# Two layers of a hybrid diffusion step, written out without a barrier, with the second layer's first modulation units moved into the first layer

## The chip, the cores and the metric

The kernel runs on one core of a Trainium2 chip. The metric is the device time of one execution in microseconds, the median of the runs. One launch computes everything.

## The reference, cut to what matters

Two token streams, a prompt of 128 tokens and a sample of 512, go through DEPTH = 2 layers with model width 1024. They share all weights, and each stream has its own condition vector, from which every layer derives 9 modulation vectors. The kernel keeps the 640 tokens of both side by side.

```python
def modulation(cvec, l):
    m = jax.nn.silu(cvec) @ w_mod[l] + b_mod[l]          # 9 vectors of 1024
    return m.reshape(cvec.shape[0], N_MOD, D_MODEL)

def layer(x, p, l, mod, ctx):
    g = p['norm_w'][l]
    def half_ffn(x, j, s):
        h = modulate(rmsnorm(x, g[2 * s]), mod[:, 3 * s], mod[:, 3 * s + 1])
        y = swiglu(h, p['ffn_w1'][l, j], p['ffn_w3'][l, j], p['ffn_w2'][l, j])
        return x + 0.5 * mod[:, 3 * s + 2][:, None] * rmsnorm(y, g[2 * s + 1])
    x = half_ffn(x, 0, 0)
    h = modulate(rmsnorm(x, g[2]), mod[:, 3], mod[:, 4])
    y, new = token_mixing(h, p, l, ctx)                  # four mixers, then w_out
    x = x + mod[:, 5][:, None] * rmsnorm(y, g[3])
    return half_ffn(x, 1, 2), new
```

The modulation depends on the condition and on w_mod[l] alone, not on x. The first feed-forward half needs its first three vectors (shift, scale, gate).

## The kernel before, in words

Everything is held feature-major: `xT` is 8 tiles of 128 features by 640 tokens. A norm of x goes like this. ScalarE (ACT) squares the eight tiles, PE sums them over the partitions with a matrix of ones (`sums`, L533 or L538), ACT takes the reciprocal root (Ln, then Exp, both at L932, the line of its helper `fn`), and `norm_in` on VectorE (DVE) scales each tile (L1310) and splits it into an upper and a lower part (ACT, then L1317). `norm_out` (L1334, L1337) scales the result of a block and adds it to x, tile by tile.

The weights come in units, one transfer each, numbered in the order in which PE uses them. There are three kinds:

- A modulation unit is 1024 KB of w_mod, 256 of its columns. PE uses it as it is (`mod`, L512, 16 matmuls with 2 output rows); the DVE copies the rows to `mrow` (L1270), PE turns them (`mod_turn`, L522, 4 matmuls), and the DVE adds the bias and stores two columns (`mod_cols`, L1276). 36 units make the nine vectors of a layer, 12 make the first three.
- An up unit (w13, 1024 KB) holds the gate and value weights of 128 hidden features. GpSimd (POOL) first splits each weight into an upper and a lower part (`split`, L454 and L459); PE makes three products of every pair (L501 to L503), 96 matmuls in all; ACT takes the Silu of the gate (L932), the DVE multiplies by the value (L1346) and splits (L1349).
- A down unit (w2, 704 KB) is treated alike and gives one output tile, copied (L1356) in group 0 and added (L1358) in group 1.

SyncE (SP) issues all weight transfers in the order of the units (`load`, L392). They go to a ring of two slots, and slot n % 2 is free once the unit two before has been split by POOL, or, for a modulation unit, used by PE. Each layer's first 12 modulation units have a ring of their own, `first_raw`, which lies in the memory of the second buffer of split weights. The split weights have two buffers as well.

Each half of the feed-forward (`ffn(s, j)`, s = 0 for the first, s = 2 for the last) runs in two groups of 11 up units and 8 down units. In the first half (s = 0) a modulation unit stands before, between and behind the up units, 12 in a group, for the last 24 of the layer. In the last half (s = 2) there are none.

The order of work at the start of a layer: the parameters `par` are loaded, then the 12 first modulation units run alone, with the squares of x beside them; after eight of them the scales are there, and `norm_step` runs between the last four. Then the products of the first up unit begin, one k tile at a time as `h_ready` rises (`first_products`).

Both layers are one piece of code in `nc.Fori(0, DEPTH)` (L376). Each engine's part of a layer is in one `nc.Block`; at the end of an iteration all semaphores are cleared and all engines meet in a barrier:

```python
        with nc.Fori(0, DEPTH) as l:
            with nc.Block() as block:
                ...
            nc.sync.sem_clear(range(nums[0], nums[-1] + 1))
            nc.all_engine_barrier()
```

Of the kernel before, what the change touches and what calls it, by code (L numbers as in the profile page):

```python
# [28 lines left out]
P = 128  # L29
# [6 lines left out]
DEPTH = 2  # L36
# [30 lines left out]
U_ALL = U_FFN[2] + 2 * GRP_U[2]  # L67
assert U_ALL == 133
# [3 lines left out]
MODS = set(range(MOD_U))  # L72
for _g in range(2):
    _n = U_FFN[0] + _g * GRP_U[0]
    MODS |= {_n + 2 * _m for _m in range(MOD_U)}
SPLIT = [n for n in range(U_ALL) if n not in MODS]
# [38 lines left out]

def build(nc, I, O):
    ctx = ExitStack()
    with ctx:
        def sb(name, words):
            return ctx.enter_context(nc.sbuf_tensor(name, [P, words], FP))  # L120

        sems = []

        def sem(name):
            s = ctx.enter_context(nc.semaphore(name))
            sems.append(s)
            return s
# [104 lines left out]
        rpb_loaded = sem("rpb_loaded")  # L232
        wa2_loaded = sem("wa2_loaded")


        first_loaded = [sem(f"first{i}_loaded") for i in range(SLOTS)]
        loaded = [sem(f"slot{i}_loaded") for i in range(SLOTS)]
        pool_hi = sem("pool_hi")
        split_done = sem("split_done")
        mrow_ready = sem("mrow_ready")  # L240
        mtr_done = sem("mtr_done")
        turn_begun = sem("turn_begun")
        split_begun = sem("split_begun")
        a_hi = sem("a_hi")
        a_lo = sem("a_lo")
        acc_add = sem("acc_add")
        y_scaled = sem("y_scaled")
        y_norm = sem("y_norm")
        dense_done = sem("dense_done")
        dense_act = sem("dense_act")  # L250
        dense_dve = sem("dense_dve")
        dense_hi = sem("dense_hi")
        spilled = sem("spilled")
        reloaded = sem("reloaded")
        y_sum = sem("y_sum")
        cat_read = sem("cat_read")
        h_hi = sem("h_hi")
        cat_hi = sem("cat_hi")
        cat_split = sem("cat_split")
        init_loaded = sem("init_loaded")  # L260
        st_out = sem("st_out")
        na_out = sem("na_out")
        m_out = sem("m_out")
        unit_done = sem("unit_done")
        unit_evac = sem("unit_evac")
        par_loaded = sem("par_loaded")
        mod_ready = sem("mod_ready")
        gate_ready = sem("gate_ready")
        sq_ready = sem("sq_ready")
        ss_done = sem("ss_done")  # L270
        rstd_ready = sem("rstd_ready")
        hmul_ready = sem("hmul_ready")
        h_ready = sem("h_ready")
        silu_done = sem("silu_done")
        x_ready = sem("x_ready")
        gate_pre = sem("gate_pre")
        gate_sp = sem("gate_sp")
        gate_log = sem("gate_log")
        gate_exp = sem("gate_exp")
        gate_t = sem("gate_t")  # L280
        gate_cols = sem("gate_cols")
        apre_done = sem("apre_done")
        asp_done = sem("asp_done")
        ad_ready = sem("ad_ready")
        ae_ready = sem("ae_ready")
        aqk_ready = sem("aqk_ready")
        akt_done = sem("akt_done")
        akt_ready = sem("akt_ready")
        lg_ready = sem("lg_ready")
        lg_sp = sem("lg_sp")  # L290
        dec_ready = sem("dec_ready")
        rot_ready = sem("rot_ready")
        rt_done = sem("rt_done")
        rt_evac = sem("rt_evac")
        qd_ready = sem("qd_ready")
        kt_ready = sem("kt_ready")
        u_done = sem("u_done")
        t_done = sem("t_done")
        s_ready = sem("s_ready")
        p_done = sem("p_done")  # L300
        wl_done = sem("wl_done")
        w_ready = sem("w_ready")
        a_done = sem("a_done")
        o_done = sem("o_done")
        ot_done = sem("ot_done")
        act_gate = sem("act_gate")
        nrm_in = sem("nrm_in")
        nrm_out = sem("nrm_out")
        fin_ready = sem("fin_ready")
        cat_t = sem("cat_t")  # L310
        cat_done = sem("cat_done")
        na_s = sem("na_s")
        na_read = sem("na_read")
        na_max = sem("na_max")
        na_e = sem("na_e")
        na_n = sem("na_n")
        na_pt = sem("na_pt")
        na_ptc = sem("na_ptc")
        na_o = sem("na_o")
        na_oc = sem("na_oc")  # L320
        cond_ready = sem("cond_ready")
        y_out = sem("y_out")
# [7 lines left out]
        slot = lambda n: n % SLOTS  # L330
        use = lambda n: 16 * ((n if n < MOD_U else n - MOD_U) // SLOTS + 1)
        SD = lambda n: PARTS * (SPLIT.index(n) + 1)
# [3 lines left out]
        R = lambda g, z, t: (g * 2 + z) * NT + t + 1  # L336
# [11 lines left out]
        def slot_ap(n, words):  # L348
            ring = first_raw if n < MOD_U else raw
            return ring[:, slot(n) * SLOT_W:slot(n) * SLOT_W + words]  # L350

        def arrival(n):
            return (first_loaded if n < MOD_U else loaded)[slot(n)]

        def split_ap(n, words):
            return w_split[SPLIT.index(n) % SLOTS][:, :, 0:words]


# [17 lines left out]
        with nc.Fori(0, DEPTH) as l:  # L376
            with nc.Block() as block:

                @block.sync
                def _(sp):  # L380
                    sp.dma_start(par[:, :], I["par"][l]).then_inc(par_loaded, 16)

                    def load(n, words, src, i=0, du=2, ds=2):


                        if MOD_U <= n < MOD_U + SLOTS:
                            pass
                        elif n - SLOTS in SPLIT:
                            sp.wait_ge(split_done, i * (ds * PARTS) + SD(n - SLOTS))
                        else:  # L390
                            sp.wait_ge(unit_done, i * du + UD(n - SLOTS))
                        sp.dma_start(slot_ap(n, words), src).then_inc(arrival(n), 16)  # L392

                    for u in range(2):
                        load(u, SLOT_W, I["w_mod"][l, u])
                    load(MOD_U + 1, SLOT_W, I["w13"][l, 0])
                    with sp.Fori(0, MOD_U // 2 - 1) as i:
                        for u in range(2):
                            load(2 + u, SLOT_W, I["w_mod"][l, i * 2 + (2 + u)], i)
                    load(MOD_U, SLOT_W, I["w_mod"][l, MOD_U])  # L400
                    for s, j in ((0, 0), (2, 1)):
                        for grp in range(2):
                            n = U_FFN[s] + grp * GRP_U[s]
                            f0 = j * FT + grp * GF_T
                            if s == 0:
                                m0 = MOD_U * (1 + grp)
                                if grp:
                                    load(n, SLOT_W, I["w_mod"][l, m0])
                                    load(n + 1, SLOT_W, I["w13"][l, f0])
                                load(n + 2, SLOT_W, I["w_mod"][l, m0 + 1])  # L410
                                with sp.Fori(0, GF_T - 1) as i:
                                    load(n + 3, SLOT_W, I["w13"][l, i + (f0 + 1)], i, ds=1)
                                    load(n + 4, SLOT_W, I["w_mod"][l, i + (m0 + 2)], i)
# [22 lines left out]
                @block.gpsimd  # L436
                def _(pool):
                    def split(n, words, i=0, du=2):


                        pool.wait_ge(arrival(n), i * (8 * du) + use(n))
                        k = SPLIT.index(n)
                        if k == 1:
                            pool.wait_ge(unit_done, UD(MOD_U - 1))
                        if k >= SLOTS and SPLIT[k - SLOTS] in AFTER:
                            pool.wait_ge(dense_done, AFTER[SPLIT[k - SLOTS]])
                        elif k >= SLOTS:
                            pool.wait_ge(unit_done, i * du + UD(SPLIT[k - SLOTS]))
                        pool.sem_inc(split_begun, 1)
                        w, src = split_ap(n, words), slot_ap(n, words)  # L450
                        step = words // PARTS
                        for q in range(PARTS):
                            at = slice(q * step, (q + 1) * step)
                            nc.gpsimd.tensor_scalar(w[:, 0, at], src[:, at], 1.0, 1.0, ALU.mult, ALU.mult)\  # L454
                                .then_inc(pool_hi, 1)
                        for q in range(PARTS):
                            at = slice(q * step, (q + 1) * step)
                            pool.wait_ge(pool_hi, i * (2 * PARTS) + (k * PARTS + q + 1))
                            nc.gpsimd.tensor_tensor(w[:, 1, at], src[:, at], w[:, 0, at].bitcast(FP), ALU.subtract)\  # L459
                                .then_inc(split_done, 1)  # L460

                    for s in (0, 2):
                        step = 2 if s == 0 else 1
                        for grp in range(2):
                            n = U_FFN[s] + grp * GRP_U[s] + step - 1
# [6 lines left out]
                            n = U_FFN[s] + (grp + 1) * GRP_U[s] - KT  # L472
# [14 lines left out]
                @block.tensor  # L487
                def _(pe):
# [1482 lines left out]
```

## Time and profile before

| | us |
|---|---|
| median of 3 runs (3286.01 to 3288.61) | 3286.97 |
| profiled execution | 3288.13 |
| its span, first to last instruction | 3286.3 |
| PE matmuls busy | 2971.4 (90%) |
| POOL busy | 1365.5 (42%) |
| DVE busy | 985.0 (30%) |
| ACT busy | 582.0 (18%) |
| mean granted TensorE clock, of full speed | 0.941 |

The profiled execution lasted 1.83 us longer than its span. Times below are in us from the start of the span. The start of layer 1 lies about in its middle: the engines leave the loop's barrier at about 1647. The granted clock is TensorE's; 1.00 is 2.4 GHz, 0.50 is 1.2 GHz.

### The profile page before, as it was taken

The page shows a single profiled execution, that of the slowest core. Times are in us where ns is not written, and L with a number is a line of the kernel's source. Part 1 is how long each engine was busy: PE and PEld are TensorE (multiplying, and loading weights), DVE is VectorE, ACT ScalarE, POOL GpSimd, SP SyncE. Part 2 cuts the span into 40 slices and gives each one's busy share as a digit, 9 for nine tenths or more (in the row PEclk, how much of TensorE's full clock was granted, in tenths as well). Part 3 has the DMA queues.
Part 4 walks back from the last instruction along what each step waited for, and adds up shares of the span by engine and source line. Part 5 has one row for each costly group of instructions (what it writes and reads, how often), then busy time and mean ns, then how long its engine had stood idle before and what let it go on. Part 6 is the DMA issues. An engine that isn't in the chain of part 4 may idle for free. (4 is left out here: it accounts for less than half of the span.)

```text
span 3286.3 us, 51128 instructions
## 1 busy us (share of the span) xinstructions
PE 2971.4 (90%) x20984; PEld 2807.7 (85%) x20984; DVE 985.0 (30%) x1589; ACT 582.0 (18%) x976; POOL 1365.5 (42%) x1556
## 2 busy tenths in 40 slices
PE   6999999798878899999779999997988787999996
PEld 3999999698877799999749999997988776999996
DVE  3110111624646531111231101116245465310112
ACT  2000001312213420011120000013121135110111
POOL 1445445333322345655314454463332223455553
PEclk7999999899888899999969999998998888999998
DMA  6332332211102111221163323322111021112111
GB/s 260 128 124 87 128 128 88 93 59 44 44 26 90 52 52 65 83 77 61 35 219 132 123 100 128 125 80 86 55 46 41 27 90 52 56 63 93 68 66 59
DMA packets 46378, 281.98 MB, mean 86 GB/s; under 512 B 5088, under 2 KB 10720, under 8 KB 20512
## 3 DMA queue, kind: packets, MB, share of 16 engines
q1 hardware_dynamic: 39024, 259.46, 22.2%
q10 hardware_dynamic: 7216, 20.60, 1.7%
q8 instruction: 96, 1.57, 0.2%
q14 instruction: 42, 0.34, 0.0%
HBM read 270.07 MB, written 9.97 MB: 85 GB/s over the span
## 5 line engine op out<-in xcount | busy, mean ns | idle before, releaser
L454 POOL TENSOR_SCALAR wsplit<-raw 128x512 fp32r<-128x512 f32 (+2 forms) x776 | 441.0, 595 | 1880.2 <-issue 856.3
L501 PE MATMUL ps<-h,wsplit 128*128 128x320 f32 (+1 forms) x3488 | 1103.4, 316 | 63.5 <-DVE rstd L1346 25.6
L502 PE MATMUL ps<-h,wsplit 128*128 128x320 f32 (+1 forms) x3488 | 1085.9, 311 | 0.0
L503 PE MATMUL ps<-h,wsplit 128*128 128x320 f32 (+1 forms) x3488 | 1085.4, 311 | 0.0
L459 POOL TENSOR_TENSOR wsplit<-raw,wsplit 128x512 fp32r<-128x512 f32 (+2 forms) x776 | 931.0, 1230 | 0.0
L501 PEld LDWEIGHTS ps<-h,wsplit 128*128 128x128 f32 (+1 forms) x3488 | 661.7, 190 | 97.0 <-DVE rstd L1346 45.7
L502 PEld LDWEIGHTS ps<-h,wsplit 128*128 128x128 f32 (+1 forms) x3488 | 662.4, 190 | 0.0
L503 PEld LDWEIGHTS ps<-h,wsplit 128*128 128x128 f32 (+1 forms) x3488 | 661.4, 190 | 0.0
L501 PE MATMUL ps<-hidden,wsplit 128*128 128x320 f32 x1408 | 435.7, 309 | 2.9 <-issue 2.9
L503 PE MATMUL ps<-hidden,wsplit 128*128 128x320 f32 x1408 | 435.1, 309 | 0.0
L502 PE MATMUL ps<-hidden,wsplit 128*128 128x320 f32 x1408 | 435.0, 309 | 0.0
L932 ACT ACTIVATE rstd<-ps 128x640 f32<-128x640 f32 x88 | 62.0, 704 | 1428.7 <-PE ps L503 1428.7
L1346 DVE TENSOR_TENSOR rstd<-rstd,ps 128x640 f32<-128x640 f32 x88 | 72.3, 821 | 769.2 <-ACT rstd L932 769.2
L501 PEld LDWEIGHTS ps<-hidden,wsplit 128*128 128x128 f32 x1408 | 264.3, 188 | 4.8 <-issue 4.8
L502 PEld LDWEIGHTS ps<-hidden,wsplit 128*128 128x128 f32 x1408 | 264.4, 188 | 0.0
L503 PEld LDWEIGHTS ps<-hidden,wsplit 128*128 128x128 f32 x1408 | 264.3, 188 | 0.0
L501 PE MATMUL ps<-wsplit,h 128*128 128x256 f32 x720 | 211.2, 293 | 0.0
L502 PE MATMUL ps<-wsplit,h 128*128 128x256 f32 x720 | 206.7, 287 | 0.0
L503 PE MATMUL ps<-wsplit,h 128*128 128x256 f32 x720 | 206.4, 287 | 0.0
L932 ACT ACTIVATE arena<-arena 128x640 f32<-128x640 f32 (+3 forms) x100 | 81.7, 823 | 383.0 <-DVE rstd L1301 191.1
L932 ACT ACTIVATE arena<-ps 128x320 f32<-128x320 f32 (+4 forms) x166 | 84.0, 511 | 361.8 <-PE ps L503 296.1
L501 PEld LDWEIGHTS ps<-wsplit,h 128*128 128x128 f32 x720 | 141.9, 197 | 2.2 <-issue 0.4
(171 smaller groups left out, 2533.2 us busy)
## 6 DMA issues: line engine op xcount, KB each, us to landing
raw<-in_w SPq DMA_DIRECT2D x88, 1024.0 KB, 4.9
raw<-in_w_mod SPq DMA_DIRECT2D x48, 1024.0 KB, 4.8
raw<-in_w SPq DMA_DIRECT2D x64, 704.0 KB, 4.1
raw<-in_w_in SPq DMA_DIRECT2D x30, 1024.0 KB, 4.8
first_raw<-in_w_mod SPq DMA_DIRECT2D x24, 1024.0 KB, 5.0
raw<-in_w_out SPq DMA_DIRECT2D x8, 768.0 KB, 4.4
spill<-xT ACTq DMA_DIRECT2D x2, 2560.0 KB, 7.6
xT<-spill ACTq DMA_DIRECT2D x2, 2560.0 KB, 13.6
```

What stands on the lines that cost most here:

```text
L454: nc.gpsimd.tensor_scalar(w[:, 0, at], src[:, at], 1.0, 1.0, ALU.mult, ALU.mult)\
L459: nc.gpsimd.tensor_tensor(w[:, 1, at], src[:, at], w[:, 0, at].bitcast(FP), ALU.subtract)\
L501: mm(out, w[0], x[0], start=first, stop=False)
L502: mm(out, w[0], x[1], start=False, stop=False)
L503: return mm(out, w[1], x[0], start=False, stop=last)
L932: return act.activation(out, in_, f, **kw)
L1346: V.tensor_tensor(halves(rstd[:, :]), halves(rstd[:, :]), acc(half(n) + 2 * BANK), ALU.mult)\
```

## The change

The loop over layers becomes a Python loop inside one block, so that each engine's code is written out for layer 0 and then for layer 1, with nothing between them. Semaphores that are counted anew in each layer exist once per layer (`Signals`); the others go on counting, with targets moved by the layer (`R`, `BLOCKS`, `PAIRS`). The modulation units 0 to 11 of layer 1 are no longer at its start: they stand in group 1 of the last half of layer 0, between its up units, in the same form as in the first half. They are numbered there as units of layer 0; for layer 1 the semaphores are raised as if its own units 0 to 11 had been done. `par` of layer 1 is loaded ahead of this group, after the last reader in layer 0 (`na_oc`). Layer 1 begins with one modulation unit, the one before its first up unit, then the norm of x as inside a layer.

```diff
-U_ALL = U_FFN[2] + 2 * GRP_U[2]
+U_ALL = [U_FFN[2] + 2 * GRP_U[2] + (MOD_U if _l + 1 < DEPTH else 0) for _l in range(DEPTH)]
+FIRST_U = [0] + [MOD_U] * (DEPTH - 1)
+def has_mods(l, s, grp):
+    return s == 0 or (s == 2 and grp == 1 and l + 1 < DEPTH)
...
-        slot = lambda n: n % SLOTS
+        slot = lambda l, n: (n + l) % SLOTS
-        R = lambda g, z, t: (g * 2 + z) * NT + t + 1
+        R = lambda l, g, z, t: ((3 * l + g) * 2 + z) * NT + t + 1
...
-        with nc.Fori(0, DEPTH) as l:
-            with nc.Block() as block:
-
-                @block.sync
-                def _(sp):
-                    sp.dma_start(par[:, :], I["par"][l]).then_inc(par_loaded, 16)
+        with nc.Block() as block:
+
+            @block.sync
+            def _(sp):
+                for l, sig in enumerate(signals):
+                    if l == 0:
+                        sp.dma_start(par[:, :], I["par"][l]).then_inc(sig.par_loaded, 16)
...
                         if MOD_U <= n < MOD_U + SLOTS:
-                            pass
+                            if l:
+                                prior = U_ALL[l - 1] - SLOTS + n - MOD_U
+                                sp.wait_ge(signals[l - 1].split_done, SD(l - 1, prior))
...
+                    else:
+                        load(MOD_U, SLOT_W, I["w_mod"][l, MOD_U])
+                        load(MOD_U + 1, SLOT_W, I["w13"][l, 0])
...
-                            if s == 0:
-                                m0 = MOD_U * (1 + grp)
+                            if has_mods(l, s, grp):
+                                lm, m0 = (l, MOD_U * (1 + grp)) if s == 0 else (l + 1, 0)
+                                if s:
+                                    sp.wait_ge(na_oc, PAIRS(l, NT * 2))
+                                    sp.dma_start(par[:, :], I["par"][lm]).then_inc(signals[lm].par_loaded, 16)
                                 if grp:
-                                    load(n, SLOT_W, I["w_mod"][l, m0])
+                                    load(n, SLOT_W, I["w_mod"][lm, m0])
                                     load(n + 1, SLOT_W, I["w13"][l, f0])
...
-                        if k == 1:
-                            pool.wait_ge(unit_done, UD(MOD_U - 1))
+                        if l == 0 and k == 1:
+                            pool.wait_ge(sig.unit_done, UD(MOD_U - 1))
+                        if l and k < SLOTS:
+                            pool.wait_ge(signals[l - 1].unit_done, UD(SPLIT[l - 1][k - SLOTS]))
...
+                    pe.sem_inc(sig.unit_done, SLOTS + FIRST_U[l])
+                    if l:
+                        pe.sem_inc(sig.mtr_done, MOD_U)
...
-                        if v and v % 2 == 0:
+                        if v % 2 == 0 and (v or l):
                             for k in range(KT):
-                                pe.wait_ge(sq_ready, KT * v + k + 1)
+                                pe.wait_ge(sig.sq_ready, KT * v + k + 1)
...
+                    if l == 0:
+                        mod(0)
+                        mod(1)
...
+                    else:
+                        mod(U_FFN[0])
+                        sums(0)
                     ffn(0, 0)
...
+                                elif l:
+                                    act.wait_ge(signals[l - 1].x_ready, 2 * KT + k + 1)
                                 last = fn(yT[:, k, :], xT[:, k, :], ACT.Square)
...
-                            q = MOD_U * (1 + grp)
-                            if s == 0:
+                            if has_mods(l, s, grp):
+                                q, m0 = (MOD_U * (1 + grp), 0) if s == 0 else (3 * MOD_U, 6 * MOD_U)
+                                if s:
+                                    dve.wait_ge(signals[l + 1].par_loaded, 16)
                                 mod_rows(n, 0)
...
+                    else:
+                        norm_in(0)
                     ffn(0, 0)
...
                     ffn(2, 1)
                     norm_out(2)
-
-            nums = sorted(s.num for s in sems)
-            assert nums == list(range(nums[0], nums[-1] + 1))
-            nc.sync.sem_clear(range(nums[0], nums[-1] + 1))
-            nc.all_engine_barrier()
+                    if l + 1 < DEPTH:
+                        mod_scales(0, signals[l + 1])
+                        mod_gates(0, signals[l + 1])
```

The rest of the diff replaces names: a semaphore `x` by `sig.x`, the functions of a unit `f(n)` by `f(l, n)`, and lists by lists per layer.

## Rows read from the trace of the kernel before

**Rows 1.** The page, part 1: busy us (share of the span) and instructions.

```profile
PE 2971.4 (90%) x20984; PEld 2807.7 (85%) x20984; DVE 985.0 (30%) x1589; ACT 582.0 (18%) x976; POOL 1365.5 (42%) x1556
```

**Rows 2.** DVE timeline at the seam: start us, us, engine, line, operation [idle].

```profile
1624.24 0.82 DVE L1358 TENSOR_TENSOR arena<-arena,ps 128x640 f32 x1 [8.12 <-PE ps L503]
...
1630.66 1.56 DVE L1334 TENSOR_TENSOR arena<-arena,rstd 128x640 f32<-128x640 f32 x2 [3.18 <-ACT rstd L932]
...
1640.97 1.55 DVE L1337 TENSOR_TENSOR xT<-xT,arena 128x640 f32<-128x640 f32 x2
1647.18 0.27 DVE L1260 MEMSET small<- 128x255 f32 x1 [4.66 <-issue]
...
1688.33 1.94 DVE L1310 SCALAR_TENSOR_TENSOR arena<-xT,gs,rstd 128x128 f32<-128x128 f32 x4
```

**Rows 3.** The timeline of ACT there: the first Silu of layer 1.

```profile
1719.93 0.70 ACT L932 ACTIVATE rstd<-ps 128x640 f32<-128x640 f32 x1 [14.77 <-PE ps L503]
```

**Rows 4.** Busy us by stretch, mid seam; after POOL: clock, DMA share, GB/s.

```profile
1629.00:1702.00 73.00, 36.10 (x258) 16.55 (x258) 36.56 (x77) 17.77 (x29) 7.26 (x8) 0.52 0.58 208
```

**Rows 5.** The chain that ended last, at the seam: start us, us, what.

```profile
1643.43 3.74 PEldq L376
...
1658.29 7.28 DMA first_raw<-in_w_mod
```

**Rows 6.** The DVE's timeline at two seams inside layer 1.

```profile
2224.47 0.82 DVE L1358 TENSOR_TENSOR arena<-arena,ps 128x640 f32 x1 [8.00 <-PE ps L503]
...
2232.38 1.96 DVE L1334 TENSOR_TENSOR arena<-arena,rstd 128x640 f32<-128x640 f32 x2 [1.80 <-ACT rstd L932]
...
2248.90 1.94 DVE L1310 SCALAR_TENSOR_TENSOR arena<-xT,gs,rstd 128x128 f32<-128x128 f32 x4 [4.26 <-ACT rstd L932]
...
2773.30 1.56 DVE L1334 TENSOR_TENSOR arena<-arena,rstd 128x640 f32<-128x640 f32 x2 [4.34 <-ACT rstd L932]
...
2789.41 1.94 DVE L1310 SCALAR_TENSOR_TENSOR arena<-xT,gs,rstd 128x128 f32<-128x128 f32 x4 [4.26 <-ACT rstd L932]
```

**Rows 7.** ACT timeline at the second seam: first Silu of the last half.

```profile
2808.56 0.70 ACT L932 ACTIVATE rstd<-ps 128x640 f32<-128x640 f32 x1 [3.51 <-PE ps L503]
```

**Rows 8.** Busy us by stretch, the start of the first products at that seam.

```profile
2792.00:2796.00 4.00, 3.33 (x14) 3.36 (x15) 4.00 (x9) 2.08 (x5) 0.00 (x0) 0.63 0.02 4
```

**Rows 9.** The timeline of POOL: the last split of layer 0.

```profile
1607.29 3.66 POOL L459 TENSOR_TENSOR wsplit<-raw,wsplit 128x352 fp32r<-128x352 f32 x4
```

**Rows 10.** SP's queue in group 1 of the first half, layer 1.

```profile
1981.42 0.33 SPq L392 DMA_DIRECT2D raw<-in_w_mod  x1
1982.57 0.33 SPq L392 DMA_DIRECT2D raw<-in_w  x1
```

**Rows 11.** The timeline of POOL there.

```profile
1990.00 2.37 POOL L454 TENSOR_SCALAR wsplit<-raw 128x512 fp32r<-128x512 f32 x4 [9.65 <-DMA raw<-in_w]
1992.33 5.02 POOL L459 TENSOR_TENSOR wsplit<-raw,wsplit 128x512 fp32r<-128x512 f32 x4
```

**Rows 12.** Busy us by stretch, last L1356 to first L1358, four groups.

```profile
329.60:521.75 192.15, 184.54 (x1364) 173.84 (x1357) 25.00 (x48) 15.87 (x22) 84.71 (x96) 1.00 0.34 126
1391.92:1556.37 164.45, 164.45 (x1123) 164.45 (x1123) 28.85 (x24) 15.91 (x22) 91.29 (x96) 1.00 0.21 74
1964.43:2156.59 192.16, 184.55 (x1364) 173.85 (x1357) 25.00 (x47) 15.86 (x22) 84.58 (x96) 1.00 0.34 126
3026.92:3191.36 164.44, 164.44 (x1123) 164.44 (x1123) 28.83 (x23) 15.90 (x22) 91.28 (x96) 1.00 0.21 74
```

**Rows 13.** What PE waited for from 1964 to 2157: us in total, times, longest.

```profile
PE ps L501 <- DVE rstd L1346: 6.7, 10, 0.7
```

**Rows 14.** The chain's last piece.

```profile
3276.78 0.73 DVEq L377
```

**Rows 15.** The DVE's timeline in that group.

```profile
1997.37 0.82 DVE L1346 TENSOR_TENSOR rstd<-rstd,ps 128x640 f32<-128x640 f32 x1 [7.50 <-ACT rstd L932]
```

More of the change, by code:

```diff
@@ L317, in build @@
[L317 to L322, printed above, removed]
+        first_loaded = [once(f"first{i}_loaded") for i in range(SLOTS)]
+        cond_ready, y_out = once("cond_ready"), once("y_out")
+        u_done = once("u_done")
+        t_done = once("t_done")
+        p_done = once("p_done")
+        a_done = once("a_done")
+        o_done = once("o_done")
+        ot_done = once("ot_done")
@@ new lines, in build @@
+        wl_done = once("wl_done")
+        w_ready = once("w_ready")
+        na_s = once("na_s")
+        na_read = once("na_read")
+        na_max = once("na_max")
+        na_e = once("na_e")
+        na_n = once("na_n")
+        na_pt = once("na_pt")
+        na_ptc = once("na_ptc")
+        na_o = once("na_o")
+        na_oc = once("na_oc")
+        split_begun = once("split_begun")
+        turn_begun = once("turn_begun")
+        gate_pre = once("gate_pre")
+        gate_sp = once("gate_sp")
@@ L324, in build @@
+        gate_log = once("gate_log")
+        gate_exp = once("gate_exp")
+        gate_t = once("gate_t")
+        gate_cols = once("gate_cols")
+        signals = [Signals(once, l) for l in range(DEPTH)]
         whole = lambda n: n if n <= U_GATES else n - N_PIECE_UNITS
@@ L346, in halves, with first, slot_ap, arrival @@
             return ap.rearrange("p (a n) -> p a n", a=2)
[L348 to L356, printed above, removed]
+        def first(l, n):
+            return l == 0 and n < MOD_U
+        def slot_ap(l, n, words):
+            ring = first_raw if first(l, n) else raw
+            return ring[:, slot(l, n) * SLOT_W:slot(l, n) * SLOT_W + words]
+        def arrival(l, n):
+            return (first_loaded if first(l, n) else signals[l].loaded)[slot(l, n)]
+        def split_ap(l, n, words):
+            at = SPLIT[l].index(n) + sum(len(SPLIT[i]) for i in range(l))
+            return w_split[at % SLOTS][:, :, 0:words]
         with nc.Block() as block:
@@ new lines, in load @@
+                        sp.dma_start(slot_ap(l, n, words), src).then_inc(arrival(l, n), 16)
+                    if l == 0:
+                        for u in range(2):
+                            load(u, SLOT_W, I["w_mod"][l, u])
+                        load(MOD_U + 1, SLOT_W, I["w13"][l, 0])
+                        with sp.Fori(0, MOD_U // 2 - 1) as i:
+                            for u in range(2):
+                                load(2 + u, SLOT_W, I["w_mod"][l, i * 2 + (2 + u)], i)
+                        load(MOD_U, SLOT_W, I["w_mod"][l, MOD_U])
+                    else:
+                        load(MOD_U, SLOT_W, I["w_mod"][l, MOD_U])
+                        load(MOD_U + 1, SLOT_W, I["w13"][l, 0])
@@ L925, in _ @@
                     ffn(2, 1)
-                    sums(5, U_ALL)
-                @block.scalar
-                def _(act):
+                    sums(5, U_ALL[l])
+            @block.scalar
+            def _(act):
+                for l, sig in enumerate(signals):
                     def fn(out, in_, f, **kw):
@@ L1188, in _ @@
                     act.drain()
-                    fn(Ga, Ga, ACT.Silu).then_inc(act_gate, 1)
+                    fn(Ga, Ga, ACT.Silu).then_inc(sig.act_gate, 1)
                     head_rstd(1)
@@ L1206, in _ @@
                     act.drain()
-                    fn(Gd, Gd, ACT.Silu).then_inc(act_gate, 1)
+                    fn(Gd, Gd, ACT.Silu).then_inc(sig.act_gate, 1)
                     drain(1)
@@ L1245, in _ @@
                     cat_upper(7)
[L1247 removed]
+                    act.wait_ge(sig.na_out, 32)
                     norm(3, 0)
@@ L1555, in _ @@
-                    norm_step(0, KT)
-                    dve.drain()
-                    mod_gates(0)
+                    if l == 0:
+                        mod_rows(0, 0)
+                        for a, b in ((0, 1), (1, 2), (2, 3)):
+                            with dve.Fori(0, b - a) as i:
+                                for u in range(2):
+                                    mod_cols(2 * a + u, 2 * a + u, i * 2)
+                                    mod_rows(2 * a + 1 + u, i)
+                            if a < 2:
+                                for k in range(a * KT // 2, (a + 1) * KT // 2):
+                                    add_square(0, k)
+                        for n in range(6, 8):
+                            mod_cols(n, n)
+                            mod_rows(n + 1, 0)
+                        dve.drain()
+                        mod_scales(0, sig)
+                        dve.wait_ge(sig.mod_ready, 1)
+                        dve.wait_ge(sig.rstd_ready, 1)
+                        for n in range(8, MOD_U):
+                            for k in (2 * n - 16, 2 * n - 15):
+                                norm_step(0, k)
+                            mod_cols(n, n)
+                            if n + 1 < MOD_U:
+                                mod_rows(n + 1, 0)
+                        norm_step(0, KT)
+                        dve.drain()
+                        mod_gates(0, sig)
+                    else:
+                        norm_in(0)
```

737 lines of the change are left out of this document (346 added, 391 removed).

## The prediction

> **What bounds the kernel now.** I read four views in this order: the busy shares, the VectorE (DVE) timeline around the seam between the two layers, the busy time by stage, and the chain of waits at the seam. TensorE (PE) is busy for 90% of the span [rows 1]; every stretch in which it is full is as long as its matmuls, and only stretches in which it is not can give time back. The seam is the largest. The last down product of layer 0 reaches the DVE at 1624.24 (L1358), and the first gate product of layer 1 reaches ScalarE (ACT) at 1719.93 (the Silu at L932) [rows 2, 3]. Between them lie 95.7 us. They consist of the last norm, until the second x tile is added at 1642.5 (1640.97 + 1.55); the end of the loop over layers, until the memset at 1647.18 of the new iteration; the first eight or so modulation units, until `norm_step` begins at 1688.33; and the norm mixed with the last units plus the first products, 31.6 us [rows 2, 3]. Over the middle of it PE has a granted clock of 0.52 and is busy 36 of 73 us [rows 4]. The chain says why: 3.74 us of it is PE's sequencer at the loop's branch (L376), and then the chain goes from one `first_raw<-in_w_mod` transfer to the next, 7.28 us for the one shown [rows 5]. No product of the layer can begin, since its scales come out of these units. So the seam is bound by transfers of modulation weights, not by PE.
>
> **What the change removes.** The seam becomes one like the two that each layer already has inside. Their rows price it:
> - Last down product to `norm_out`: this part is the same code as now, 1624.24 to 1630.66, 6.4 us [rows 2]. The seam after the first feed-forward half has 2224.47 to 2232.38, 7.9 us, with four small scale products and a POOL split beside it [rows 6].
> - `norm_out`, squares, `sums`, reciprocal root, first `norm_step`: 2232.38 to 2248.90 is 16.5 us, 2773.30 to 2789.41 is 16.1 us [rows 6]. I take 16.3. The new `mod_scales(0)`, `mod_gates(0)` and the memset come in here behind the last x tile. They cost nothing: the DVE waits there 4.26 us for the root (the bracket of the row at 2789.41), and the three are a fraction of that (the memset takes 0.27 [rows 2]). Without the cover they would cost under 1 us.
> - First `norm_step` to the first Silu: 2789.41 to 2808.56, 19.15 us [rows 6, 7]. It is that same up unit of 96 matmuls, released one k at a time.
>
> New seam: 6.4 + 16.3 + 19.15 = 41.9 us. Removed: 95.7 - 41.9 = 53.8 us. With the seam at 2224.47 as it stands (24.4 + 19.15 = 43.6) it would be 52.1. Both are my bounds, widened by 1 us for the clock: PE comes into the first products at 0.63 in the like seam [rows 8], and the one modulation unit that stays in the seam (`mod(U_FFN[0])` between `sums(5)` and `sums(0)`) can only keep it busier. That unit itself lies in the time in which PE waits for the squares; it takes about 2 us there, and a delay could reach the path only if its transfer came late. That transfer is now issued as soon as the last but one weight of layer 0 is split, before the seam.
>
> Could the weights of the first up unit be late in place of the scales? The last split of layer 0 ends at 1607.29 + 3.66 = 1611.0 [rows 9]; this releases the transfer. Transfer and split together take 14.8 us (issue at 1982.57, split until 1992.33 + 5.02 = 1997.35) [rows 10, 11], so they are done by about 1626. First use is at about 1624.2 + 6.4 + 16.3 + 2 = 1649. 23 us to spare. The second up unit's transfer stands behind the next modulation unit's on the SP queue, which waits for `mod(U_FFN[0])` on PE, about 1633; plus 14.8 is 1648, and it is wanted about 1666. Its split falls beside the norm on the DVE, which I price at 0 to 0.5 us.
>
> **What it adds.** Group 1 of the last feed-forward half of layer 0 takes the form of group 1 of the first half. This price is in the trace exactly, since both forms run in both layers. From the last copy of group 0 (L1356) to the first addition of group 1 (L1358) the form with units takes 192.15 and 192.16 us, the form without 164.45 and 164.44 [rows 12]. The difference is 27.7 us. It is complete: 1364 - 1123 = 241 more matmuls, which is 12 units of 16 and 12 turns of 4; 20.1 us more PE busy time; and 7.6 us in which PE waits, of which 6.7 are ten waits for the evacuation at L1346 [rows 12, 13]. The clock is 1.00 in all four. The parameter load (`par`) is new on the SP queue ahead of the group's first unit. It is 389 KB against a 1024 KB weight, and its wait (`na_oc`) was met before the half began: 0 to 1 us, taken as 0. The DVE wait for it stands before `mod_rows`, with the whole of the last down units as cover. The downs that follow, and layer 1 from its first Silu, keep their code.
>
> **Small parts.** The second end of the loop over layers (0.73 us on the DVE [rows 14]), the semaphore clear and a barrier go at the end: 0 to 0.9, I take 0.3. Code addresses: layer 1 is now other code than layer 0. Between like points, 329.60 to 1391.92 in layer 0 and 1964.43 to 3026.92 in layer 1, the stretches are 1062.3 and 1062.5 us [rows 12]. Code met for the first time therefore cost nothing against code met again, and I price the second copy at 0, with bounds -1 and +2.
> The Trainium skill ("Runtime: NRT & Kernel Launch", Instruction fetch mechanics) has a branch outside the prefetched window stall until its page is fetched, while straight code streams. The one such stall that the rows show is L376, and it is in the seam's 95.7 already; by the rule nothing is added for the longer program.
>
> **Sum.** Against the profiled execution's own 3288.13 us (span 3286.3): 3288.13 - 53.8 + 27.7 - 0.3 = 3261.7. The median of the runs is 1.16 lower, 3286.97, so the forecast is 3260.6 us, 26.4 us or 0.8% less.
>
> **Rivals.**
> 1. *The weight ring of the new group becomes late.* With units in a group, the up weights of all units use one slot of the ring. Issue of `w13` at 1982.57, split done at 1997.35, and PE may go on at 1997.37 + 0.82 = 1998.19: a margin of only 0.8 us [rows 10, 11, 15]. A transfer that takes 2 us longer than those 7.4 (1990.00 - 1982.57) would add about 1.2 us to each of 11 periods, 13 us in all, so about 3274. For it: the margin is thin. Against it: both groups of both first halves keep it with the same traffic, to 0.01 us.
> 2. *The same ring decides the sign.* If transfer and split of each `w13` took 3.2 us longer than now, each of 11 periods would grow by 2.4, 26.4 us, and eat the gain. At a transfer of 12.5 us instead of 7.4, 4.3 us per period are exposed, +47 us: 3260.6 + 47 = 3308, slower. It starts to be slower at 10.6 us. Against it: the stretch has just these two streams, and they would have to differ only because they are behind other down units.
> 3. *The seam does not shrink to the like one*, since one late thing (root, first weights, a sequencer coming into new code on a slow fetch as at L376) holds it. One fetch stall of 3.7 on each of two engines in turn gives +7: 3268. To be without gain the seam would have to keep 68 us, a late weight of 26 us, against 23 us of margin before the first microsecond counts: 3287.
>
> **How the numbers follow.** Forecast 0.85 (of it 3258.5 to 3264 is its own spread, from 52.1 - 1 to 54.2 + 1 removed and -1 to +2 for the rest). Rival 1: 0.05. Rival 3: 0.06, 0.02 of it without gain. Rival 2: 0.03. Something unseen that gives more: 0.01. The range is 3257 to 3267, which leaves out the rivals' far ends. A change under 0.2% (6.6 us) cannot be told from none. Faster by more: 0.94, within: 0.03, slower: 0.03.
>
> **What would show it.** From the last L1358 of layer 0 to the first Silu of layer 1: 41.9 us (40.5 to 44.5), with no stretch of transfers before `norm_step`. Group 1 of that half: 192.2 us at clock 1.00, with ten waits of 0.67 at L1346; any wait there for POOL's split speaks for rivals 1 and 2. No 3.7 us stall of a sequencer in between. `first_raw<-in_w_mod` falls from 24 to 12 transfers and `raw<-in_w_mod` rises from 48 to 60. Layer 0 up to that group and layer 1 after its first Silu keep their lengths to 1 us. I am wrong if the seam is over 48 us or the group over 196.

## The result: 0.45% faster, where 0.8% was forecast

The changed kernel takes 3273.91 us (median of 6 runs, 3269.7 to 3276.25), the kernel before in the same sessions 3288.74 us. The ratio is 0.9955 with a 95% interval of 0.9942 to 0.9968: 14.8 us less, where 26.4 were forecast. The time lies above my range of 3257 to 3267.

The profiled execution took 3275.47 us (span 3273.7), 12.7 less than the one of before. The page has PE as busy as before, for the 12 units (192 matmuls) and their 12 turns have only changed places:

```profile
PE 2971.1 (91%) x21012; PEld 2812.1 (86%) x21012; DVE 972.3 (30%) x1580; ACT 580.3 (18%) x974; POOL 1361.0 (42%) x1556
```

Its list of DMA issues shows that the units have moved as the change says:

```profile
raw<-in_w_mod SPq DMA_DIRECT2D x60, 1024.0 KB, 4.9
...
first_raw<-in_w_mod SPq DMA_DIRECT2D x12, 1024.0 KB, 5.0
```

Lines of the changed file are new: the down additions are L1398 (before L1358), the multiply L1386 (L1346), `norm_out` L1374 and L1377 (L1334, L1337), `norm_step` L1350 and L1357 (L1310, L1317), ACT's helper L964 (L932), a modulation unit L538 (L512), `sums` L559 for eight tiles and L564 for the accumulated one (L533, L538), POOL's split L477 and L482 (L454, L459).

**The price of the units came out exactly.** Busy time by stretch in the changed kernel, the group with the moved units (it answers to the second row of [rows 12]), and what PE waited for in it (it answers to [rows 13]):

```profile
1393.27:1585.43 192.16, 184.54 (x1364) 173.84 (x1357) 25.00 (x48) 15.88 (x22) 84.87 (x96) 1.00 0.34 126
```

```profile
PE ps L527 <- DVE rstd L1386: 6.7, 10, 0.7
PE ps L527 <- issue: 0.7, 1, 0.7
```

192.16 against 164.45 is 27.7 us, at a granted clock of 1.00 and with no wait for a split. So rivals 1 and 2, which let these weights come late, did not happen.

**The seam did not.** The DVE's timeline there (it answers to [rows 2]), then ACT's, with the last two squares, the Ln of the root and the first Silu of layer 1 (to [rows 3]):

```profile
1653.30 0.82 DVE L1398 TENSOR_TENSOR arena<-arena,ps 128x640 f32 x1 [8.12 <-PE ps L529]
...
1660.45 1.56 DVE L1374 TENSOR_TENSOR arena<-arena,rstd 128x640 f32<-128x640 f32 x2 [3.90 <-ACT rstd L964]
...
1670.75 1.55 DVE L1377 TENSOR_TENSOR xT<-xT,arena 128x640 f32<-128x640 f32 x2
...
1684.15 5.01 DVE L1350 SCALAR_TENSOR_TENSOR arena<-xT,gs,rstd 128x128 f32<-128x128 f32 x4 [11.40 <-ACT rstd L964]
```

```profile
1671.60 1.47 ACT L964 ACTIVATE arena<-xT 128x640 f32<-128x640 f32 x2 [0.73 <-DVE xT L1377]
...
1682.41 0.79 ACT L964 ACTIVATE rstd<-ps,small 128x640 f32<-128x640 f32 x1 [8.03 <-PE ps L559]
...
1706.58 0.70 ACT L964 ACTIVATE rstd<-ps 128x640 f32<-128x640 f32 x1 [3.96 <-PE ps L529]
```

It is 53.3 us from the first row to the Silu, where 41.9 were forecast and 95.7 stood before. Two things differ from the like seams in [rows 6]: the DVE waits 11.40 us for the root in place of 4.26, and the first four `norm_step` operations last 5.01 us in place of 1.94. The longer wait begins on PE. Its timeline:

```profile
1656.69 2.09 PE L564 MATMUL ps<-rstd,const 128*128 128x320 f32 x4 [3.54 <-DVE rstd L1341]
1671.05 1.89 PE L538 MATMUL ps<-raw,cond 128*2 128x256 f32 x16 [12.27 <-DVEq L1294]
1672.86 9.51 PE L559 MATMUL ps<-arena,const 128*128 128x320 f32 x32
```

PE sat idle for 12.27 us ahead of the one modulation unit in the seam, until L1294, and `sums(0)` stands behind that unit on PE. The unit writes its rows to PSUM, the memory that PE writes its results to, and `unit_evac` counts the units whose place there the DVE has emptied, so PE waits for it (kernel.py, cut):

```python
                    def mod(n, i=0, du=2):
                        pe.wait_ge(arrival(l, n), i * (8 * du) + use(n))
                        pe.wait_ge(sig.unit_evac, i * du + (whole(n) + 1))
                        ...
```

For layer 1 the DVE raises this counter in one go, as the first line of its code for the layer: L1294, `dve.sem_inc(sig.unit_evac, 2 + FIRST_U[l])`. The view of that line (its two executions, the second at 1670.9, and who waited for it):

```profile
L1294 DVEq EVENT_SEMAPHORE  x2: 21/21/21, 7.4 to 1670.9; - x2
...
  PE ps L538: 12.3, 1
```

The DVE's queue comes to it only with the last x tiles of layer 0. By then all squares but two were made. `sums(0)` could not run beside them. It came in one piece, out of an idle time, and took 9.51 us, the first of it at half clock (busy us by stretch; the third value from the end is the clock):

```profile
1660.00:1672.00 12.00, 0.95 (x12) 0.42 (x16) 11.55 (x16) 5.23 (x8) 0.00 (x0) 0.50 0.00 0
1672.00:1676.00 4.00, 4.00 (x21) 2.21 (x11) 0.74 (x4) 2.36 (x3) 0.00 (x0) 0.73 0.45 152
```

The half clock is the smaller part of this. From 1674.40 on the matmuls of `sums(0)` begin 0.27 us apart, at a granted clock of 1.00, and 32 of them at that pace would last 8.8 us (an estimate from this trace). So the clock cost about 0.7 of the 9.51 us. The rest is work that the like seams hide behind the squares.

The four longer `norm_step` operations stand beside a split on POOL. SP issued the second up weight only at 1673.68, since the modulation transfer ahead of it waits for the late unit on PE. SP's queue, then POOL's timeline:

```profile
1672.99 0.33 SPq L405 DMA_DIRECT2D raw<-in_w_mod  x1
1673.68 0.34 SPq L405 DMA_DIRECT2D raw<-in_w  x1
```

```profile
1680.59 2.37 POOL L477 TENSOR_SCALAR wsplit<-raw 128x512 fp32r<-128x512 f32 x4 [28.06 <-DMA raw<-in_w]
1682.92 5.43 POOL L482 TENSOR_TENSOR wsplit<-raw,wsplit 128x512 fp32r<-128x512 f32 x4
```

### The profile page after: what moved, and what is told of

The parts are those of the page before. It is cut to its first block, busy times and chain, and to the rows that moved or that the text cites. A ratio compares the mean times of both kernels' runs of the same rounds, so it can differ in the third digit from the quotient of the medians.

```text
span 3273.7 us, 50932 instructions
## 1 busy us (share of the span) xinstructions
PE 2971.1 (91%) x21012; PEld 2812.1 (86%) x21012; DVE 972.3 (30%) x1580; ACT 580.3 (18%) x974; POOL 1361.0 (42%) x1556
## 4 chain that ended last, share of the span: by engine, by line
PE 84%; DVE 8%; ACT 3%; issue 2%; DMA 1%; DVEq 1%; POOL 0%; ACTq 0%; SPq 0%
PE ps L527 25%; PE ps L529 24%; PE ps L528 24%; PE ps L559 2%; ACT rstd L964 2%; PE ps L753 1%; PE ps L696 1%; ACT arena L964 1%; DVE rstd L1386 1%; PE ps L716 1%; PE ps L736 1%; DMA first_raw<-in_w_mod 1%; DVE arena L1350 1%; PE ps L548 1%; PE ps L760 1%
## 5 line engine op out<-in xcount | busy, mean ns | idle before, releaser
L477 POOL TENSOR_SCALAR wsplit<-raw 128x512 fp32r<-128x512 f32 (+2 forms) x776 | 443.6, 600 | 1872.3 <-issue 831.2
L482 POOL TENSOR_TENSOR wsplit<-raw,wsplit 128x512 fp32r<-128x512 f32 (+2 forms) x776 | 924.4, 1224 | 0.0
L964 ACT ACTIVATE rstd<-ps 128x640 f32<-128x640 f32 x88 | 62.0, 705 | 1443.9 <-PE ps L529 1443.9
L1386 DVE TENSOR_TENSOR rstd<-rstd,ps 128x640 f32<-128x640 f32 x88 | 72.3, 821 | 733.8 <-ACT rstd L964 733.8
L964 ACT ACTIVATE arena<-arena 128x640 f32<-128x640 f32 (+3 forms) x100 | 81.7, 823 | 384.1 <-DVE rstd L1341 190.3
L964 ACT ACTIVATE arena<-ps 128x320 f32<-128x320 f32 (+4 forms) x166 | 84.0, 512 | 360.9 <-PE ps L529 295.8
```

What stands on the lines that cost most here:

```text
L964: return act.activation(out, in_, f, **kw)
L1386: V.tensor_tensor(halves(rstd[:, :]), halves(rstd[:, :]), acc(half(n) + 2 * BANK), ALU.mult)\
```

## Theories and experiments

*A, the late counter*: the unit waits for `unit_evac`, `sums(0)` waits behind it, and so does the next modulation transfer on SP with the second up weight behind that, whose split then meets the first `norm_step`. *B, the clock*: `sums(0)` is slow whenever it starts. *C, new code*: the engines come slowly into layer 1's copy. Seam means in the table the last down addition of layer 0 to the first multiply of layer 1, 0.73 to 0.74 us more than to the Silu. The expectations of the changed kernel again, e1 and e2 give the seam to the Silu, the later ones to the multiply. Mixing is the time from the last multiply of the first half to the first of the last half, both layers together, in the profiled execution. Medians are over 5 runs or more. Ratios are against the kernel before, run beside each (3288.2 to 3288.7).

| kernel | seam | mixing | median | ratio (95%) |
|---|---|---|---|---|
| before | 96.4 | 1327.9 | 3288.7 | 1 |
| changed | 54.0 | 1331.0 | 3273.9 | 0.9955 (0.9942 to 0.9968) |
| a0_changed_again | 53.9 | 1330.0 | 3273.4 | 0.9955 (0.9941 to 0.9968) |
| e1_early_counters | 44.7 | 1328.6 | 3263.3 | 0.9927 (0.9913 to 0.9940) |
| e2_sums_first | 43.7 | 1325.8 | 3260.5 | 0.9914 (0.9901 to 0.9928) |
| e2_again | 43.2 | 1329.3 | 3263.4 | 0.9920 (0.9907 to 0.9934) |
| e3_split_at_norm | 47.4 | 1328.2 | 3266.5 | 0.9935 (0.9922 to 0.9949) |
| e4_block_per_layer | 61.6 | 1328.3 | 3280.3 | 0.9978 (0.9969 to 0.9987) |
| e5_unrolled_only | 82.2 | 1328.9 | 3273.4 | 0.9956 (0.9942 to 0.9969) |
| e6_early_w13_ahead | 48.1 | 1329.3 | 3267.3 | 0.9935 (0.9922 to 0.9949) |
| e7_sums_w13_ahead | 47.9 | 1328.8 | 3266.5 | 0.9936 (0.9923 to 0.9950) |
| e8_split_behind_norm | 43.2 | 1328.9 | 3264.6 | 0.9927 (0.9914 to 0.9941) |

**The changed kernel again.** No edit.

> The changed kernel once more, unedited, as the base of the others. Seam (last L1398 of layer 0 to the first Silu of layer 1) 53.3 us as in its first profile; time 3270 to 3276 us. The token mixing was 2.1 us longer in layer 0 and 1.0 us longer in layer 1 than before the change. If that is the run's own scatter, this profile shows other amounts (between -2 and +3 in each layer); if it belongs to the new code, it shows +2.1 and +1.0 again to within 0.3.

The seam came again to 0.1 us (53.15 to the Silu). Its parts moved more: the Ln stands 10.0 us behind the last square in place of 9.3, and the first four norm steps take 4.25 us in place of 5.01. The mixing was 1.1 us longer than before the change in layer 0 and 1.0 us in layer 1, so neither of the two forms of the expectation is met cleanly; over the twelve profiles its sum moves between 1325.8 and 1331.0, and `e2_again`, an unedited repeat, moved it by 3.5. I count the 3.2 us of the first profile as scatter between executions.

**Counters early.**

```diff
-                    dve.sem_inc(sig.unit_evac, 2 + FIRST_U[l])
-                    if l:
-                        dve.sem_inc(sig.mrow_ready, MOD_U)
-                        dve.sem_inc(sig.acc_add, KT)
-                    dve.sem_inc(sig.a_lo, 1)
+                    if l == 0:
+                        for i, t in enumerate(signals):
+                            dve.sem_inc(t.unit_evac, 2 + FIRST_U[i])
+                            if i:
+                                dve.sem_inc(t.mrow_ready, MOD_U)
+                                dve.sem_inc(t.acc_add, KT)
+                            dve.sem_inc(t.a_lo, 1)
```

> The DVE raises layer 1's counters (unit_evac and the others) at the very start instead of at the head of its code for layer 1. Theory A (late counter: the one modulation unit in the seam waits for it, stands ahead of sums(0) on PE, and holds the second up weight back, whose split then collides with the first norm_step): all 11 us come back, seam 41.5 to 44, time 10 to 12 us under the changed kernel run beside it. Theory B (the clock: sums(0) takes 9.5 us because PE comes out of a long idle time at 0.50, whenever it starts): sums(0) starts with the squares but ends 2 to 3 us behind the last one; seam 46 to 48, 5 to 7 us gained. Theory C (the engines come slowly into code that they meet at the seam): under 2 us gained.

9.2 us of seam and 10.1 us of time came back. PE's timeline in this kernel: the unit now runs in the idle time, and `sums(0)` goes along with the squares.

```profile
1658.66 1.89 PE L538 MATMUL ps<-raw,cond 128*2 128x256 f32 x16 [2.08 <-ACT rstd L964]
1661.37 11.33 PE L559 MATMUL ps<-arena,const 128*128 128x320 f32 x32 [0.82 <-ACT arena L964]
```

It ends at 1672.70, 1.8 us behind the last square (1669.40 + 1.47 = 1670.87), as in the like seams (1.7 us in the one at 2224.47). That speaks for A and against C, which had under 2 us of gain, and against B, which had 46 to 48 us of seam. To the Silu the seam is 44.0 us, A's upper end. What is left shows on the DVE, and POOL beside it:

```profile
1674.47 4.09 DVE L1352 SCALAR_TENSOR_TENSOR arena<-xT,gs,rstd 128x128 f32<-128x128 f32 x4 [3.49 <-ACT rstd L964]
```

```profile
1668.14 4.22 POOL L477 TENSOR_SCALAR wsplit<-raw 128x512 fp32r<-128x512 f32 x4 [17.26 <-DMA raw<-in_w]
1672.32 5.43 POOL L482 TENSOR_TENSOR wsplit<-raw,wsplit 128x512 fp32r<-128x512 f32 x4
```

The split still meets the first norm steps, only with its end.

**sums(0) ahead of the unit**, counters late as in the change.

```diff
                     else:
-                        mod(U_FFN[0])
                         sums(0)
+                        mod(U_FFN[0])
```

> Counters late as in the change, but PE makes sums(0) before the modulation unit in the seam. Theory A: sums(0) ends about 1.8 us behind the last square, 7.6 us come back; the second up weight is issued even later, so its split (7.4 us) falls into the norm steps and costs 1 to 3 us of them; seam 45 to 48, 5 to 8 us gained. Theory B: sums(0) no sooner done than 3 us behind the squares: 5 us gained. Theory C: under 2 us.

The seam to the Silu is 43.0, better than the 45 to 48 that I gave it, and the time 12.9 us under the changed kernel's, where I had 5 to 8. So A has the direction right and its price for the split wrong. The split began 8.7 us after the first norm step and ran beside the later ones, but it was the split that lost time, 8.19 us in its first part in place of 2.37. The DVE's steps kept their 1.00 us a pair, and only the last pair took 1.48. POOL's timeline:

```profile
1683.82 8.19 POOL L477 TENSOR_SCALAR wsplit<-raw 128x512 fp32r<-128x512 f32 x4 [32.25 <-DMA raw<-in_w]
1691.98 5.01 POOL L482 TENSOR_TENSOR wsplit<-raw,wsplit 128x512 fp32r<-128x512 f32 x4
```

The counter is as late as in the change, and nothing waits for it: PE comes to the unit only after the root. So the harm is not in the counter by itself but in what PE has queued behind the unit that waits for it.

**The split held until the root.** `e1_early_counters`, with this in POOL's `split`:

```diff
+                        if l and k == 1:
+                            pool.wait_ge(sig.rstd_ready, 1)
```

> e1_early_counters, and POOL begins the second split of layer 1 only when the root of the norm is there, so that it starts with the first norm_step. If POOL's split is what made the first four L1350 last 5.0 us instead of 1.9, they last 4 to 5 us here and 1.9 to 2.2 in e1_early_counters, and this kernel is 2 to 3.5 us slower than that one. If not, both are the same to 0.5 us in the seam.

It is 3.2 us slower than e1, and its seam 2.7 us longer, as expected for POOL as the cause. The first four steps themselves missed: 3.44 us here, where I had 4 to 5, and 4.09 in e1, where I had 1.9 to 2.2, as e1's split met them too. The loss fell on the steps behind them. The DVE's timeline shows three stretches of 3.0 to 3.4 us where 1.0 to 1.9 belong:

```profile
1672.49 3.44 DVE L1354 SCALAR_TENSOR_TENSOR arena<-xT,gs,rstd 128x128 f32<-128x128 f32 x4 [4.00 <-ACT rstd L966]
1675.85 3.02 DVE L1361 SCALAR_TENSOR_TENSOR h<-arena,modS,h 128x128 fp32r<-128x128 f32 x2
1678.79 3.04 DVE L1354 SCALAR_TENSOR_TENSOR arena<-xT,gs,rstd 128x128 f32<-128x128 f32 x2
```

**The split early.** In group 0 of layer 1, SP issues the up weight first. `e6` has this with the counters early, `e7` with `sums(0)` first.

```diff
+                                if l and s == 0 and grp == 0:
+                                    load(n + 3, SLOT_W, I["w13"][l, f0 + 1])
+                                    load(n + 2, SLOT_W, I["w_mod"][lm, m0 + 1])
+                                    with sp.Fori(0, GF_T - 2) as i:
+                                        load(n + 5, SLOT_W, I["w13"][l, i + (f0 + 2)], i, ds=1)
+                                        load(n + 4, SLOT_W, I["w_mod"][lm, i + (m0 + 2)], i)
...
```

> e1_early_counters, and in group 0 of layer 1 SP issues each up weight ahead of the modulation weight, so that the second split of layer 1 runs about 1657 to 1665 beside the adding of x tiles instead of until 1677.7. If the split's meeting with the first norm_step is what e1 still loses (L1352 x4 4.1 us instead of 1.9), these are back at 1.9 and the seam falls from 44.7 to 42.6 to 43; if the DVE loses as much beside the x tiles (L1376, L1379), the seam stays at 44 to 45.

> e2_sums_first with the same order on SP: PE makes sums(0) first and the second split runs early. Seam 42.6 to 43.5, that is 0 to 1 us under e2_sums_first (43.7), whose split met the end of the norm steps. Whole time by theory A: 3259 to 3262 us, scatter of the token mixing included.

Both missed, by 3.4 and 4.2 us of seam in the wrong direction (against e1 and e2). The norm steps are back at 1.94, but the x tiles pay more. The DVE's timeline in e6, and POOL's:

```profile
1661.32 1.88 DVE L1387 TENSOR_TENSOR xT<-xT,arena 128x640 f32<-128x640 f32 x1
1663.12 1.88 DVE L1384 TENSOR_TENSOR arena<-arena,rstd 128x640 f32<-128x640 f32 x1
1664.93 1.88 DVE L1387 TENSOR_TENSOR xT<-xT,arena 128x640 f32<-128x640 f32 x1
1666.73 0.81 DVE L1384 TENSOR_TENSOR arena<-arena,rstd 128x640 f32<-128x640 f32 x1
1667.47 0.81 DVE L1387 TENSOR_TENSOR xT<-xT,arena 128x640 f32<-128x640 f32 x1
```

```profile
1658.88 7.25 POOL L490 TENSOR_TENSOR wsplit<-raw,wsplit 128x512 fp32r<-128x512 f32 x4
```

While POOL's four TENSOR_TENSORs run, the DVE's follow one another every 1.80 us instead of 0.74, and POOL's own take 1.81 us each instead of 1.26: they take turns.

The Trainium skill ("SBUF — State Buffer", SBUF: two separate sides) says so: a DVE operation with two SBUF inputs and a GpSimd operation that reads SBUF exclude one another, each for a whole instruction. The trace nearly agrees: a turn of one operation each takes 1.80 us, where the two alone take 0.74 and 1.26, 2.00 in sum.

**The split behind the norm.** `e7_sums_w13_ahead`, with POOL's second split of layer 1 waiting for `h_ready` at 7.

> e7_sums_w13_ahead, with POOL's second split of layer 1 held back until the seventh h tile is ready, so that it meets neither the x tiles nor the first norm steps. If the meeting of POOL's split with the DVE is all that e7 lost against the like seams, the x tiles go back to 0.74 us each and the seam from 47.9 to 42.7 to 43.7, at or up to 1 us under e2_sums_first run beside it. If the split comes too late for PE, the second multiply of layer 1 comes over 17 us after the first instead of 16.7.

> e2_sums_first once more: seam 43.7 to within 0.3 us; the token mixing of the two layers together between 1325 and 1331 us, as in the profiles so far. If its 1325.8 of the first profile belongs to this program and not to the run, it comes again to within 1 us.

The seam falls from 47.9 to 43.2 by this one wait, so the meeting of the two engines was all that e7 had lost. But the second multiply comes 18.0 us after the first, not 16.7, since the split is now late, and in time e8 is no better than e2 run beside it (3264.6 and 3263.4). What PE waited for from 1693 to 1714, in e8 and then in e2_again:

```profile
PE ps L537 <- POOL wsplit L492: 1.2, 1, 1.2
```

```profile
PE ps L527 <- POOL wsplit L482: 0.9, 1, 0.9
```

So e2 itself has no slack left here: its first profile has no such wait, its second has 0.9 us, and its second multiply comes at 17.7 instead of 16.7. e2_again has the seam of e8, 0.5 us off its first profile where I had 0.3, and its mixing did not come again to 1 us.

**The two parts of the change, one at a time.** `e4` puts each layer into a block of its own (`for at_l in range(DEPTH): with nc.Block() as block:`), units moved. `e5` leaves the 12 units at the start of layer 1 (`has_mods` is `s == 0`, the start of layer 0 used for both, `first_raw` loaded when the last down unit is done), one block, no loop.

> The changed kernel with one block per layer, so that all engines meet at the end of layer 0; the modulation units stay moved, no loop over layers. No engine can issue or signal for layer 1 before the last x tile. From the rows so far: last L1398 to the end of norm_out 18.3 us, meeting about 1, transfer 7.5, modulation unit 1.9, sums(0) at 0.50 clock 9.6, root 1.7, norm to the first multiply 20: seam (last addition of a down product to the first multiply at the L1386 line) 58 to 61 against 54.0 in the changed kernel, 4 to 7 us slower than it. If the late counter already costs as much as a barrier would, as theory A reads, no more than 7; if the barrier is worth more than the counter (rival), over 10.

> The other part alone: layers written out without a barrier, but the 12 modulation units of layer 1 stay at its start, alone, as before the change. Their first transfers now start when PE has done the last down unit and the branch stall of 3.7 us is gone, but the DVE can only copy the first row of units when norm_out is done (18.4 us after the last addition instead of 30.5). Seam 96.4 - 12.1 = 84.3, up to 4 less since two units are already there: 80 to 85, so 12 to 16 us gained against the kernel before, and no cost in group 1 of the last half (164.4 us). A rival that lays the worth of the change on the barrier alone has about 26 - here; one that lays it on the loop's branch alone has 4.

Both came as expected but for 0.6 us of e4's seam (61.6; 6.9 us slower than the changed kernel). In e4 SP issues for layer 1 only at 1669.07, and PE's unit waits for that transfer, not for a counter:

```profile
1673.79 1.88 PE L539 MATMUL ps<-raw,cond 128*2 128x256 f32 x16 [18.68 <-DMA raw<-in_w_mod]
```

e5 is as fast as the whole change, 3273.4 us both. Leaving out the barrier and the loop gave 14.8 us. Moving the units on top of it gave nothing, since it took 28.2 us from the seam (82.2 to 54.0) and put 27.7 into the group. With `sums(0)` first the move takes 38.5 to 39.0 us from the seam, and only then pays.

## Why the prediction was wrong, by its own steps

- **The added group**: right to 0.01 us, 27.7. So were its ten waits and the clock. A like stretch of the same kernel, read by its ends, priced it. (The 241 more matmuls are one more than the 240 of 12 units and 12 turns; the stretch, not the count, carried the price.)
- **Small parts**: taken as 0.3, with bounds up to 0.9. The time between the last DVE operation and the end of the span fell by 0.7 us; the first multiply of layer 0 came 0.8 us sooner, within what it moves between profiles (83.9 to 86.0). Layer 1 as new code cost nothing: its first half took 424.6 us in both kernels.
- **The step that failed** is in "What the change removes": "That unit itself lies in the time in which PE waits for the squares; ... a delay could reach the path only if its transfer came late." The prediction took the overlap of the unit and of `sums(0)` with the squares for granted. The unit's transfer was in time, but the counter `unit_evac`, raised by the DVE at the head of layer 1, came late. The diff ahead of the prediction shows PE's `sem_inc`, but I never asked when the DVE's comes.
- **What it cost**: 53.8 us were to go, and 42.4 went. By the terms of the sum, 6.4 measured 7.15, 16.3 measured 23.7 and 19.15 measured 22.4. The 11.4 us divide by cause about so. The Ln stands 9.3 us behind the last square (1682.41 - 1673.07) where the seam at 2224.47 has 1.8, which is 7.6; e1 and e2 took this away in two different ways. The first norm steps took 5.01 us and not 1.94, which is 3.1; e3, e6, e7 and e8 moved this part. `norm_out` began 7.15 us after the last addition instead of 6.42, which is 0.7; this is not the change's own, since it is 6.48 in the changed kernel again, and 6.48 and 7.14 in e2's two profiles. The seam of 53.3 us is over the 48 that the prediction named as its own sign of being wrong.
- **The split beside the norm** was priced at 0 to 0.5 us. It was 3.1 in the change, 2.1 in e1, and 4.2 to 4.7 where it met the x tiles. The row at 2224.47 in [rows 6] had the sign of it, a slower first part "with four small scale products and a POOL split beside it", which I took as a bound and did not follow.
- **Rival 3** was the right kind, a late thing in the seam, at 0.06. I had looked for it among transfers and code and not among counters. Its +7 was short of the 11.4.
- **The stated spread** was too narrow for its own terms: 51.1 to 55.2 us removed and -1 to +2 for the rest make about 3258 to 3265, not 3258.5 to 3264, and the 54.2 comes from none of the rows (with 16.1 in place of 16.3 it is 54.0). This did not decide anything.
- **Scatter**: the median difference is 14.8 where seam and group give 14.7. The mixing's 3.2 us are in the first profile, not shown to belong to the change.

With this step mended, the forecast is met. To the Silu, the seam is 43.0 us in e2 and 42.4 in e2_again, where 41.9 were forecast. The time fell by 27.6 and 25.1 us in the two sessions (ratios 0.9914 and 0.9920, each known to about 4 us either way), where 26.4 were forecast. Both are faster than the changed kernel and the kernel before.

## What to carry to other kernels

When a stage is pulled ahead, list every counter that its first instruction waits for and find where each is raised, in the queue order of the engine that raises it: the one `sem_inc` here, which stood on the DVE's queue behind all of `norm_out`, came 17.6 us after the last down addition and held up the unit that waited for it and all that PE had queued behind. Where an instruction may wait, put what is on the critical path ahead of it on that engine. And place POOL work in time as carefully as DVE work: a split that "has slack" for PE was free here only where it did not land on a DVE stretch that the next stage waited for.

## What the runs showed of the hardware

A POOL TENSOR_TENSOR and the DVE's two-input operations take turns: 0.74 us becomes 1.80 us a piece for the DVE, 1.26 becomes 1.81 for POOL, and one POOL split placed on the x tiles costs the seam 4.2 to 4.7 us (e7 against e2 and e8). POOL's one-input part suffers too: four operations take 8.19 us instead of 2.37 beside the norm steps in e2, while these keep their 1.00 us a pair. In e3, where both begin together, both lose: 2.86 us instead of 2.37 on POOL, 3.44 instead of 1.94 on the DVE (its last step met the two-input part). What decides between the two outcomes is not shown.

The 32 ones-matmuls of `sums(0)` took 9.5 us in one piece, behind a stretch of 12 us (1660 to 1672) in which PE was busy for 0.95 us at a granted clock of 0.50. In the first 1.5 us they begin 0.5 to 0.7 us apart, then 0.27 at a clock of 1.00, so that the clock accounts for about 0.7 us of the 9.5. Begun with the squares they were hidden but for 1.8 us.
